# The recurrent layer's inputs: key norms by token, mixtures inside the norm, low products spread among the values

## The reference, cut to what matters

```
xs[n] = h + (h' - h) * mu[n]                       # n = r, k, v, w, a, g: the mixtures
r, k, v = xs[0] @ Wr, xs[1] @ Wk, xs[2] @ Wv       # 1024 x 1024 each
w = w0 + tanh(xs[3] @ wd1) @ wd2                   # 1024 -> 64 -> 1024
a = sigmoid(a0 + (xs[4] @ wa1) @ wa2)              # 1024 -> 64 -> 1024
g = sigmoid(xs[5] @ wg1) @ wg2                     # 1024 -> 160 -> 1024
kk = k * k_k
kk = kk / max(sqrt(sum over a head's 64 (kk * kk)), 1e-12)     # 16 heads of 64
k_mod = k * (1 + (a - 1) * k_a)
```

## Time and profile before

| | us |
|---|---|
| median of 3 runs | 4322.08 |
| lowest, highest | 4319.68, 4322.27 |
| the profiled execution | 4317.04 |
| its span | 4315.2 |
| PE busy | 4166.0 (97%) |
| DVE busy | 1942.0 (45%) |
| POOL busy | 1112.1 (26%) |
| ACT busy | 701.1 (16%) |
| mean granted TensorE clock | 0.968 of full |

### The profile page before, as it was taken

One profiled execution on the slowest core, in us unless ns is written; L12 is line 12 of the kernel. 1 busy time (PEld: TensorE's weight loads), 2 busy tenths in 40 slices (PEclk: granted clock), 3 DMA queues, 4 the chain that ended last, 5 costly groups with the idle time before them and its releaser, 6 DMA issues.

```text
span 4315.2 us, 43399 instructions
## 1 busy us (share of the span) xinstructions
PE 4166.0 (97%) x17144; PEld 2943.7 (68%) x17144; DVE 1942.0 (45%) x3582; ACT 701.1 (16%) x1452; POOL 1112.1 (26%) x960
## 2 busy tenths in 40 slices
PE   7999999999999999999999999999999989989998
PEld 3448884445588744788833488888886447838887
DVE  3446663246377622433245443333334754454432
ACT  2321110113311100100014310010001321211000
POOL 0003430002344200344300134434442051003443
PEclk9999999998999999999999999999999899989999
DMA  3114443210154442222210122222222132112222
GB/s 119 49 54 168 173 174 135 93 64 30 40 189 175 152 143 88 72 88 86 95 49 20 40 88 88 83 74 88 88 90 66 59 112 59 36 40 78 88 83 73
DMA packets 128105, 387.61 MB, mean 90 GB/s; under 512 B 37984, under 2 KB 41056, under 8 KB 117152
## 3 DMA queue, kind: packets, MB, share of 16 engines
q1 hardware_dynamic: 112592, 302.56, 21.4%
q10 hardware_dynamic: 13824, 75.50, 4.7%
q0 software_dynamic: 1488, 6.78, 0.4%
HBM read 376.40 MB, written 8.39 MB: 89 GB/s over the span
## 4 chain that ended last, share of the span: by engine, by line
PE 93%; DVE 4%; ACT 2%; issue 1%; DMA 0%; POOL 0%; DVEq 0%; ACTq 0%; POOLq 0%
PE bank L762 92%; DVE temporary L2620 1%; PE bank L1202 1%; DVE normed L1911 1%; ACT normed L1449 0%; PE bank L1109 0%; DMA vector_columns<-in_vectors_dram 0%; ACT temporary L1449 0%; ACT area_b L1449 0%; PE bank L1331 0%; DVE area_a L2433 0%; ACT squares L1449 0%; DVE rstd L1926 0%; ACT L1449 0%; DVE temporary L2144 0%
## 5 line engine op out<-in xcount | busy, mean ns | idle before, releaser
L762 PE MATMUL bank<-normed,weight_ring 128*128 128x256 f32 (+2 forms) x3312 | 1025.7, 464 | 17.6 <-DVE normed L1917 5.8
L762 PEld LDWEIGHTS bank<-normed,weight_ring 128*128 128x128 f32 (+1 forms) x3312 | 635.6, 194 | 367.9 <-issue 285.2
L762 PE MATMUL bank<-area_a,weight_ring 128*128 128x512 f32 (+1 forms) x1776 | 636.5, 515 | 8.2 <-issue 8.2
L762 PE MATMUL bank<-area_b,weight_ring 128*128 128x256 f32 (+3 forms) x2000 | 589.2, 441 | 5.9 <-issue 2.8
L762 PEld LDWEIGHTS bank<-area_a,weight_ring 128*128 128x128 f32 x1776 | 339.7, 192 | 282.1 <-issue 259.9
L695 POOL TENSOR_TENSOR area_d<-weight_ring 128x512 f32<-128x512 f32 (+1 forms) x92 | 114.7, 1246 | 1571.0 <-PE bank L762 816.6
L762 PEld LDWEIGHTS bank<-area_b,weight_ring 128*128 128x128 f32 (+2 forms) x2000 | 375.5, 188 | 186.8 <-issue 145.9
L762 PE MATMUL bank<-area_b 128*128 128x256 f32 (+2 forms) x1584 | 345.0, 378 | 16.2 <-ACT area_d L1449 16.2
L762 PEld LDWEIGHTS bank<-area_b 128*128 128x128 f32 (+1 forms) x1584 | 287.1, 194 | 61.0 <-ACT area_d L1449 16.9
L762 PE MATMUL bank<-area_b,area_d 128*128 128x256 f32 x1440 | 326.1, 379 | 0.0
L762 PEld LDWEIGHTS bank<-area_b,area_d 128*128 128x128 f32 x1440 | 273.8, 190 | 37.5 <-issue 0.2
(11 more groups left out here) (296 smaller groups left out, 4788.7 us busy)
## 6 DMA issues: line engine op xcount, KB each, us to landing
weight_ring<-in_weights_dram SPq DMA_DIRECT2D x429, 512.0 KB, 4.6
area_b<-in_weights_dram ACTq DMA_DIRECT2D x48, 1024.0 KB, 4.9
weight_ring<-in_weights_dram SPq DMA_DIRECT2D x35, 1024.0 KB, 4.9
area_b<-in_weights_dram ACTq DMA_DIRECT2D x48, 512.0 KB, 6.3
weight_ring<-in_weights_dram SPq DMA_DIRECT2D x40, 384.0 KB, 4.4
...
```

What stands on the lines that cost most here:

```text
L762: i = pe.matmul(out, lhsT, rhs, start=start, stop=stop)
```

## The change

- The eight k mixtures are made between the norm's scalings, each when ACT has shifted its block. The a and g mixtures are made in turn within the key loop, the v mixtures behind it; g mixtures now lie in B.
- Key norms by token: PE takes 128 tokens of the squared keys as the stationary operand and two columns of `halves` as the moving one, so that the sums come with tokens on partitions, 128x64 numbers for all blocks (`KEY_SUMS`). DVE takes their maximum, ACT the root, DVE the reciprocal, once (`KEY_NORM`). POOL widens them to 128x512 for each block in turn (into SQ), PE turns them back with four 128x128 matmuls against the unit matrix (`spread`), and DVE multiplies (`unit_key`).
- `key_square(j - 1)` stands behind key product j, where `key_square(j - 2)` stood.
- g is projected ahead of w2 and a2; w2, a2 and a spread take turns for each j.
- The low products stand in pieces, one chunk behind every second matmul of value products 1, 2, 3 and 5. ACT does decays j + 2 ahead of the copy of value block j, one each. SP stores the groups ahead of weight tiles 10, 11, 11 and 12.
- The second inversion waits for the last spread in place of the last a2.

```diff
@@ -111,9 +111,12 @@
-RW_PARTS = {"k": (64, 64), "w1": (192, 8), "a1": (200, 8), "w2": (224, 8), "a2": (232, 8), "g": (208, 16),
+RW_PARTS = {"k": (64, 64), "w1": (192, 8), "a1": (200, 8), "g": (208, 16), "w2": (224, 8), "a2": (232, 8),
             "v": (128, 64), "r": (0, 64)}
-RW_PRODUCTS = {"k": 0, "w1": 8, "a1": 9, "w2": 10, "a2": 18, "g": 26, "v": 28, "r": 36}
+RW_PRODUCTS = {"k": 0, "w1": 8, "a1": 9, "g": 10, "w2": 12, "a2": 13, "v": 28, "r": 36}
+LOW_BESIDE = {1: 0, 2: 1, 3: 2, 5: 3}
@@ -538,11 +541,19 @@
         def rw_in(what, j=0):
-            return AT["rw_in"][0] + RW_PRODUCTS[what] + j
+            return AT["rw_in"][0] + RW_PRODUCTS[what] + (2 * j if what in ("w2", "a2") else j)
-            return AT["rw_in"][1] + {"square": 0, "low": 8, "bonus": 40}[what] + j
+            return AT["rw_in"][1] + {"spread": 0, "low": 8, "bonus": 40}[what] + j
+        def mixed_with(what, k):
+            place = ("k", "w1", "a1", "g", "v", "r").index(what)
+            return 2 * DB + 2 * k + place - 1 if what in ("a1", "g") else DB * place + k + 1
+        KEY_SUMS, KEY_NORM = bank[4][:, 0:64], D[:, 9, 416:480]
@@ -638,8 +649,13 @@
             for n, (_, _) in enumerate(STREAM):
-                if rw_tile + 10 <= n <= rw_tile + 13:
-                    store_low(n - rw_tile - 10)
+                if n == rw_tile + 10:
+                    store_low(0)
+                if n == rw_tile + 11:
+                    store_low(1)
+                    store_low(2)
+                if n == rw_tile + 12:
+                    store_low(3)
                 if n == rw_tile + 15:
@@ -729,7 +745,10 @@
                 low, x = small_blocks[h], inverses[h]
-                full(po, rw_in(*(("k", 0), ("a2", 7))[h]))
+                if h == 0:
+                    full(po, rw_in("k", 0))
+                else:
+                    sfull(po, rw_in_small("spread", 7))
                 po.memset(x, 0.0).then_inc(S("inverse_step"), 1)
@@ -749,6 +768,15 @@
                 return steps + 63
+            by_token = KEY_NORM.rearrange("p (t h) -> p t h", h=16)
+            po.wait_ge(S("key_rstd"), 1)
+            for j in range(DB):
+                if j >= 2:
+                    sfull(po, rw_in_small("spread", j - 2))
+                po.tensor_copy(SQ[:, j % 2, :].rearrange("p (t h f) -> p t h f", h=2, f=64),
+                               by_token[:, :, 2 * j:2 * j + 2].unsqueeze(3).to_broadcast([P, NB, 2, 64]))                    .then_inc(S("key_widened"), 1)
@@ -1218,42 +1246,59 @@
-                at["w"] = w0 + RW_PARTS[("r", "k", "v", "w1", "a1", "g")[n]][0]
-                place = ("k", "w1", "a1", "g", "v", "r").index(("r", "k", "v", "w1", "a1", "g")[n])
+                what = ("r", "k", "v", "w1", "a1", "g")[n]
+                at["w"] = w0 + RW_PARTS[what][0]
                 for j in range(rows):
-                    project(xs, DB, (lambda k: pe.wait_ge(S("mixed"), DB * place + k + 1)) if j == 0 else settled)
+                    project(xs, DB, (lambda k: pe.wait_ge(S("mixed"), mixed_with(what, k))) if j == 0 else settled)
                     small_of(j)
             def key_square(j):
+                pe.wait_ge(S("kk_square"), j + 1)
+                for t in range(NB):
+                    mm(KEY_SUMS[:, 16 * t + 2 * j:16 * t + 2 * j + 2], SQ[:, j % 2, t * P:(t + 1) * P],
+                       const("halves")[:, 0:P:64], True, True, S("key_summed") if t == NB - 1 else None)
+            def spread(j):
                 s = small()
-                pe.wait_ge(S("kk_square"), j + 1)
-                mm(sbank(s)[:, :], const("halves"), SQ[:, j % 2, :], True, True, small_full)
+                pe.wait_ge(S("key_widened"), j + 1)
+                for t in range(NB):
+                    mm(sbank(s)[:, t * P:(t + 1) * P], SQ[:, j % 2, t * P:(t + 1) * P],
+                       const("ident"), True, True, small_full if t == NB - 1 else None)
-            def low_products(g):
-                pe.wait_ge(S("rw_scaled"), 2 * g + 2)
-                for c in range(NB):
-                    ss = [small(), small()]
-                    for b in range(2):
-                        for half in range(2):
-                            rows, j = slice(64 * half, 64 * half + 64), 2 * g + b
-                            mm(sbank(ss[half])[:, b * P:(b + 1) * P], B[rows, 8 + j, chunk(c)], B[rows, j, chunk(c)],
-                               True, True, small_full if b else None)
-            rw_project(1, lambda k: A[:, k, :], 8, lambda j: key_square(j - 2) if j >= 2 else None)
-            rw_project(3, lambda k: A[:, 16 + k, :], 1, lambda j: key_square(6))
-            rw_project(4, lambda k: B[:, 16 + k, :], 1, lambda j: key_square(7))
-            for n, what in enumerate(("w2", "a2")):
-                at["w"] = w0 + RW_PARTS[what][0]
-                done(pe, rw_in(("w1", "a1")[n]))
-                for j in range(8):
+            def low_product(g, c):
+                if c == 0:
+                    pe.wait_ge(S("rw_scaled"), 2 * g + 2)
+                ss = [small(), small()]
+                for b in range(2):
+                    for half in range(2):
+                        rows, j = slice(64 * half, 64 * half + 64), 2 * g + b
+                        mm(sbank(ss[half])[:, b * P:(b + 1) * P], B[rows, 8 + j, chunk(c)], B[rows, j, chunk(c)],
+                           True, True, small_full if b else None)
+            rw_project(1, lambda k: A[:, k, :], 8, lambda j: key_square(j - 1) if j >= 1 else None)
+            rw_project(3, lambda k: A[:, 16 + k, :], 1, lambda j: key_square(7))
+            rw_project(4, lambda k: B[:, 16 + k, :], 1, lambda j: None)
+            rw_project(5, lambda k: B[:, 8 + k, :], 2, lambda j: None)
+            for j in range(8):
+                for n, what in enumerate(("w2", "a2")):
+                    at["w"] = w0 + RW_PARTS[what][0] + j
+                    done(pe, rw_in(("w1", "a1")[n]))
                     project(lambda k: D[:, n, :], 1, settled, rows=64)
-            rw_project(5, lambda k: A[:, 16 + k, :], 2, settled)
-            rw_project(2, lambda k: A[:, k, :], 8, lambda j: low_products(j // 2) if j % 2 else None)
+                spread(j)
+            at["w"] = w0 + RW_PARTS["v"][0]
+            for j in range(8):
+                m = product()
+                for k in range(DB):
+                    if j == 0:
+                        pe.wait_ge(S("mixed"), mixed_with("v", k))
+                    mm(pbank(m)[:, :], weight(), A[:, k, :], k == 0, k == DB - 1, product_full if k == DB - 1 else None)
+                    if k % 2 and j in LOW_BESIDE:
+                        low_product(LOW_BESIDE[j], k // 2)
             rw_project(0, lambda k: H[:, k - 1, :] if k else RB[:, :], 8, lambda j: bonus(j - 2) if j >= 2 else None)
@@ -1770,32 +1815,31 @@
             norm(10, 6)
-            for j in range(DB + 2):
+            for j in range(DB + 1):
                 if j < DB:
                     took(a(A[:, 8 + j, :], pbank(m)[:, :], ACT.Identity), m)
-                if 1 <= j <= DB:
+                if j >= 1:
                     act.wait_ge(S("kk_raw"), j)
                     if j >= 3:
-                        sfull(act, rw_in_small("square", j - 3))
+                        act.wait_ge(S("key_summed"), j - 2)
                     a(SQ[:, (j - 1) % 2, :], B[:, j - 1, :], ACT.Square).then_inc(S("kk_square"), 1)
-                if j >= 2:
-                    sdone(act, rw_in_small("square", j - 2))
-                    a(TM[:, j % 2, :], TM[:, j % 2, :], ACT.Sqrt).then_inc(S("kk_root"), 1)
             for what, out, rows, func in (("w1", D[0:64, 0, :], 64, ACT.Tanh), ("a1", D[0:64, 1, :], 64, ACT.Identity)):
                 took(a(out, pbank(m)[0:rows, :], func), m)
-            for what, first, name in (("w2", 16, "rwkv_w0"), ("a2", 8, "rwkv_a0")):
-                for j in range(DB):
-                    m = rw_in(what, j)
-                    full(act, m)
-                    took(a(B[:, first + j, :], pbank(m)[:, :], ACT.Sigmoid, bias=vec(name, j)), m)
+            act.wait_ge(S("key_most"), 1)
+            a(KEY_NORM, KEY_NORM, ACT.Sqrt).then_inc(S("key_root"), 1)
             for j, (out, rows) in enumerate(((PT[:, 0, :], P), (PT[0:32, 1, :], 32))):
                 took(a(out, pbank(m)[0:rows, :], ACT.Sigmoid), m)
+            for j in range(DB):
+                for what, first, name in (("w2", 16, "rwkv_w0"), ("a2", 8, "rwkv_a0")):
+                    m = rw_in(what, j)
+                    full(act, m)
+                    took(a(B[:, first + j, :], pbank(m)[:, :], ACT.Sigmoid, bias=vec(name, j)), m)
@@ -1809,27 +1853,28 @@
-            def copy_low(g):
-                for c in range(NB):
-                    n = NB * g + c
-                    if n >= 2:
-                        act.wait_ge(S(f"low_stored{n % 2}"), 16 * (n // 2))
-                    for half in range(2):
-                        s = rw_in_small("low", 2 * n + half)
```

(79 more changed lines are left out.)

## The result

The changed kernel takes 4329.33 us (median of 20 runs, 4322.65 to 4332.03), the kernel before 4320.41 in the same comparison. The ratio is 1.0020, with a 95% interval of 1.0013 to 1.0027: **slower by some 9 us** (6 to 12 by the interval). But the whole interval lies above no change, and the sum said slightly down.

A forecast was written before the change was run, and what follows sets the result against it. PE was taken as the bound (93% of the chain that ended last), losing time in waits and at half clock. Terms gave +0.7 up to the values and -2.6 in them: -1.9, so 4320.2 us, range 4309 to 4331.

The forecast's parts named there:

- Mixtures inside the norm: In the norm, DVE alternates scalings and mixtures without waiting for ACT's last shift: -0.9 us.
- Pause and half clock out: Around w2, a2 and gate products: the 5.1 us pause and the half-clock time behind it go, -21.9 us.
- Key squares: Key products: squares' own work unchanged; PE waits 2.8 us before the first square, 1.4 before six others (+8.4).
- The clock there: Half clock behind the key squares' waits: +1.7 us at the first, +3.4 over the six others.
- Norms by token: Beside w2 and a2: eight spreads at 0.9 us each on PE, +7.2 us (ends 7.2 and 8.4).
- The chain in front: Before the first spread: maximum, root, reciprocal and widening take 3 to 4 us, hidden under PE's work, 0.
- The values: Value products with low products: 86.7 us instead of 89.3, -2.6 us.
- Group 3's wait: In the values, PE's wait ahead of low-product group 3, behind value product 4's copy and decays 7: 3.6 to 4.4 us.
- the signs that I named: Signs of being right: full clock, no pause from w1 to last spread; named waits; values 84 to 90 us.
- Rival 2: Faster: clock stays full in the new, shorter waits, 11.6 us fall away, 4308.6 us; chance 0.21.
- Rival 3: Slower: w2, a2 and spreads run at half clock, 21 us of work doubles, 4341 us; chance 0.08.
- Rival 4: Slower: half clock behind each key square and for longer, 4337 us at 3.2 us each; chance 0.07.

The follow-up runs named there:

- b_g_first: Kernel before with only the mixtures inside the norm and the gate products ahead of w2 and a2; 4296.00 us, ratio to before 0.9942.
- a_lag2: Changed kernel with the key squares two products behind again instead of one; 4309.15 us, ratio to the kernel before 0.9979.
- a_rows128: Changed kernel with w2 and a2 products reading all 128 rows instead of 64; 4327.61 us, ratio to the kernel before 1.0013.
- a_pieces_two: Changed kernel with low products two pieces at a time, behind matmuls 4 and 8 of the value product; 4325.84 us, ratio to the kernel before 1.0015.
- a_stage3: Changed kernel with three buffers instead of two for ACT's copies of low products ahead of SP's stores; 4327.84 us, ratio to the kernel before 1.0017.
- a_decays: Changed kernel with only ACT's order altered: decays 5 and 7 ahead of copies they stood behind; 4320.58 us, ratio to the kernel before 1.0002.

## Why the prediction was wrong

Its steps, against the changed kernel's trace and the runs:

- *Mixtures inside the norm*, -0.9: about -0.7. *Pause and half clock out*, -21.9: right (b_g_first, -22.6 up to the values, with the mixtures).
- *Key squares*: the first wait 2.54 for 2.8; the six others 1.5 each (9.23 - 7.72) for 1.4. *The clock there*, 5.1: three stretches of 1.7 each, 5.1, the right amount by luck: I had one behind the first wait, where there is none, and two behind the other six, where there are three. a_lag2 takes the squares' waits and the clock together away, 16.7 us for my 16.3.
- **Norms by token, +7.2: failed, it is +10.2.** I took 0.86 or 0.9 for the spread and nothing for its place. A turn is 3.00 us, 0.42 more than its matmuls. a_rows128 shows that the 3 us of all eight turns are the two changes between 64 and 128 rows in each. The range that I gave for this term (7.2 to 8.4) was too narrow. The chain in front was hidden, as said: the first block is widened 12 us before the first spread.
- So the values start 4.4 us later than before, not 0.7: 3.0 of the 3.7 between them from the turns, the rest from the squares and the mixtures. This alone did not decide the result: a_rows128 takes the 3.1 us out, and the stretch is still 7.9 us longer than before.
- **The values, -2.6: failed, they are +3.9.** The 6.4 us between them, product by product: product 1 with its group ends 27.8 us behind the start for 25.9; product 2 with its group, which waits for nothing, takes 10.24 for 9.1; product 3 takes 17.9 for 15.7; 4 and 5 take 23.4 for 22.3. The cost of a piece in its place is in each of them (entered at 0.5 or 0.55, 0.84 measured: 2.56 - 1.72), and a_pieces_two shows it alone. In product 1 both waits ended as said (12.1 and 19.0 us behind the start for 12.1 and 19.1), but what lies behind the second, entered at 5.1 of work and 1.7 of clock, took 8.8: 5.8 of work (three pieces of 0.64 and twice 1.92 for two value matmuls) and 3.0 of clock. In product 3 the wait itself is 1.9 longer than its 4.2: decays 5 on ACT stand behind a copy that a store holds up. a_stage3 took 0.7 of these 1.9 away, a_decays the wait altogether. Group 3's wait, 4.54 for 3.6 to 4.4, was about right. Of the signs that I named, the values at 93.2 us lie outside 84 to 90, and a spread in its turn costs 1.27 us, not 0.9; no pause and full clock from w1 to the last spread, and the places of the waits, came as said.
- *The rivals.* Rival 2 (full clock in the shorter waits) is false: behind 2.54 us the clock stayed, behind several of 1.2 and behind 3.39 it fell. Rival 3 is false: w2 and a2 ran at 1.00. Rival 4 has the right place but not the price: the waits and the clock at the squares cost what the sum said. None of them was the case that came: slower by small amounts that I had entered at nothing or too low, namely the changes between 64 and 128 rows (in the turns, and by their size in the pieces too), the store that holds up the copy ahead of decays 5 on ACT, and more half clock in product 1. I gave slower a chance of 0.15.

Why slower, then? Moving the gate products, with the mixtures inside the norm, gains 22.6 us up to the values, and this is shown without the rest of the change. Three other parts of the same change take it back and more: the squares one block behind (16.7 us), the spreads (10.2), and pieces in turn with copies that bind ACT (16.5 of the values, where whole groups in the change's places would have gained 12.6 on before).

Not settled: how far the pieces' price is the same change of rows as in the turns, which no run with 128 rows in the pieces tests; what sets which of several equal waits of 1.2 us is followed by a stretch at 0.50, and how much of the values' half clock is due to each wait.
